# The rings of the split weights are moved by 16 bytes against the activations

## The reference

```python
def swiglu_ffn(h, w_gate_up, w_down):
    gate, up = jnp.split(h @ w_gate_up, 2, axis=-1)
    return (jax.nn.silu(gate) * up) @ w_down

def reference(x, ...):
    h = x
    for i in range(DEPTH):                      # DEPTH = 2
        kind, j = i % N_MIXERS, i // N_MIXERS
        if kind == 0:
            h = h + stick_breaking_mixer(rmsnorm(h, sb_norm[j]), sb_w_qkv[j], sb_w_o[j])
        elif kind == 1:
            h = h + chunked_gmlp_mixer(rmsnorm(h, gm_norm[j]), gm_w_in[j], gm_v_norm[j],
                                       gm_w_s[j], gm_b_s[j], gm_w_o[j])
        ...
        h = h + swiglu_ffn(rmsnorm(h, ffn_norm[i]), ffn_w_gate_up[i], ffn_w_down[i])
    return rmsnorm(h, final_norm)
```

## Time and profile before

| | |
|---|---|
| median of 2 runs | 2072.2 us (2070.47 to 2073.94) |
| the profiled execution | 2069.99 us |
| its span, first to last instruction | 2068.3 us |
| TensorE matmul busy | 2058.8 us |
| VectorE busy | 1430.0 us |
| ScalarE busy | 1011.4 us |
| granted TensorE clock, mean | 0.999 |
| moved by DMA | 402.47 MB, mean 195 GB/s |

### The profile page before, as it was taken

The page is one execution under the profiler, slowest core; times in us unless marked ns, Lnnn a source line. Parts: engine busy times, 40 slices in busy tenths (PEclk is TensorE's granted clock), DMA queues, the critical chain, the costliest instruction groups (busy, mean ns, idle before and its releaser), DMA issues.

```text
span 2068.3 us, 27155 instructions
## 1 busy us (share of the span) xinstructions
PE 2058.8 (100%) x9279; PEld 1721.7 (83%) x9279; DVE 1430.0 (69%) x1822; ACT 1011.4 (49%) x1285; POOL 16.4 (1%) x30
## 2 busy tenths in 40 slices
PE   9999999999999999999999999999999999999998
PEld 7888888888888888888888888888888888888887
DVE  7787787867766677666557887877766677665454
ACT  6677765544444444444445444554444444444443
POOL 1000000000000000000000000000000000000000
PEclk9999999999999999999999999999999999999999
DMA  8555655666666666556567665566666666655554
GB/s 276 183 188 158 188 187 172 199 198 195 195 191 200 195 197 195 195 194 201 195 196 211 193 203 186 191 194 204 195 191 202 194 198 196 191 198 201 194 194 152
DMA packets 207419, 402.47 MB, mean 195 GB/s; under 512 B 12336, under 2 KB 13056, under 8 KB 206976
## 3 DMA queue, kind: packets, MB, share of 16 engines
q1 hardware_dynamic: 206496, 398.11, 61.8%
q0 software_dynamic: 688, 3.18, 0.4%
q10 hardware_dynamic: 176, 0.40, 0.1%
HBM read 399.55 MB, written 2.10 MB: 194 GB/s over the span
## 4 chain that ended last, share of the span: by engine, by line
PE 99%; issue 0%; ACT 0%; DVE 0%; POOLq 0%; POOL 0%; DVEq 0%; ACTq 0%
PE acc L1101 65%; PE acc L1109 32%; PE tp L1205 1%; PE tp L1185 1%; PE tp L1334 0%; PE acc L1151 0%; PE tp L1117 0%; PE acc L1144 0%; PE acc L1377 0%; PE acc L1375 0%; PE acc L1376 0%; ACT xT L382 0%; PE tp L1193 0%; DVE h L1070 0%; ACT junk L640 0%
## 5 line engine op out<-in xcount | busy, mean ns | idle before, releaser
L672 DVE TENSOR_TENSOR w_lo<-raw,w_hi 128x1024 fp32r<-128x1024 f32 x750 | 915.7, 1224 | 560.5 <-ACT w_hi L364 558.6
L364 ACT ACTIVATE w_hi<-raw 128x1024 fp32r<-128x1024 f32 x750 | 791.7, 1059 | 894.7 <-PE acc L1109 889.9
L1101 PE MATMUL acc<-w_hi,xT 128*128 128x512 f32 x4080 | 996.9, 385 | 0.0
L1101 PEld LDWEIGHTS acc<-w_hi,xT 128*128 128x128 f32 x4080 | 762.6, 187 | 148.2
L1109 PE MATMUL acc<-w_lo,xT 128*128 128x512 f32 x2040 | 539.0, 385 | 0.0
L1109 PEld LDWEIGHTS acc<-w_lo,xT 128*128 128x128 f32 x2040 | 381.9, 187 | 74.1
L1101 PE MATMUL acc<-w_hi,hid_lo 128*128 128x512 f32 x944 | 364.4, 386 | 0.0
L1101 PE MATMUL acc<-w_hi,hid_hi 128*128 128x512 f32 x944 | 362.3, 384 | 0.0
L1109 PE MATMUL acc<-w_lo,hid_hi 128*128 128x512 f32 x944 | 249.5, 385 | 0.0
L1101 PEld LDWEIGHTS acc<-w_hi,hid_lo 128*128 128x128 f32 x944 | 176.9, 187 | 36.4
L1109 PEld LDWEIGHTS acc<-w_lo,hid_hi 128*128 128x128 f32 x944 | 176.7, 187 | 34.4
(11 more groups left out here) (117 smaller groups left out, 428.3 us busy)
## 6 DMA issues: line engine op xcount, KB each, us to landing
raw<-in_ffn_w_gate_up SPq DMA_DIRECT2D x352, 512.0 KB, 4.5
raw<-in_ffn_w_down SPq DMA_DIRECT2D x176, 512.0 KB, 3.7
raw<-in_sb_w_qkv SPq DMA_DIRECT2D x95, 512.0 KB, 4.3
raw<-in_gm_w_in SPq DMA_DIRECT2D x64, 512.0 KB, 4.5
raw<-in_sb_w_o SPq DMA_DIRECT2D x32, 512.0 KB, 4.2
raw<-in_gm_w_o SPq DMA_DIRECT2D x32, 512.0 KB, 4.1
h<-in_x SPq DMA_DIRECT2D x3, 512.0 KB, 8.8
gain_bc<-in_gm_v_norm POOLq DMA_DIRECT2D x1, 1024.0 KB, 6.2
```

The costliest lines, as they stand in the source:

```text
L364: nc.scalar.activation(w_hi[:, p % RING], raw[:, p % RING], ACT.Copy).then_inc(hi_ready, 1)
L672: nc.vector.tensor_tensor(w_lo[:, p % RING], raw[:, p % RING], w_hi[:, p % RING].bitcast(f32), ALU.subtract).then_inc(lo_ready, 1)
L1101: nc.tensor.matmul(swept(acc_at(chunk, r)), part[:, kt, rs], swept(w_hi[:, p % RING, k]), start=(kt == 0 and part is hi), stop=False)
```

## The change

`w_hi` and `w_lo` were two tensors of SBUF. Now they are two views into one tensor `parts`, which is 32 bytes longer than both together; w_hi begins 16 bytes (SKEW = LINE = 4 elements) into it and w_lo right behind w_hi. parts begins where w_hi began. raw, xT and h don't move, and region keeps a multiple of 512 bytes from parts. So the moving tiles begin 16 bytes beyond the place modulo 512 at which the stationary tiles begin. The tensors between w_lo and lead_in move by 32 bytes. No instruction is added, removed or put elsewhere.

```diff
         raw = sb("raw", [P, RING, KP, CH])
-        w_hi = sb("w_hi", [P, RING, KP, CH], f32r)
-        w_lo = sb("w_lo", [P, RING, KP, CH], f32r)
+        SKEW, SIZE = LINE, RING * KP * CH
+        parts = sb("parts", [P, 2 * SIZE + 2 * LINE], f32r)
+
+        def ring(first):
+            return parts[:, first:first + SIZE].rearrange("p (s k n) -> p s k n", s=RING, k=KP)
+
+        w_hi = ring(SKEW)
+        w_lo = ring(SKEW + SIZE)
         gate = sb("gate", [P, RT, CH])
...
         used_up_to = nc.lookup_mloc(moments).addr + 32
-        lead_in = sb("lead_in", [P, (nc.lookup_mloc(w_hi).addr - used_up_to) % CH // 4])
+        lead_in = sb("lead_in", [P, (nc.lookup_mloc(parts).addr - used_up_to) % CH // 4])
         region = sb("region", [P, 2 * KF * S])
         R0 = nc.lookup_mloc(region).addr
-        assert (R0 - nc.lookup_mloc(w_hi).addr) % CH == 0
+        assert (R0 - nc.lookup_mloc(parts).addr) % CH == 0
```

## The result

| | before | after |
|---|---|---|
| median of 2 runs | 2072.2 us | 2095.5 us (2095.32 to 2095.76) |
| span of the profiled execution | 2068.3 us | 2093.6 us |
| ratio to before | | 1.0113, 95% interval 1.0069 to 1.0156 |

The kernel became 1.1% slower, by 25.3 us in the spans. That is inside the stated range and within 2%, but it is a change: the interval leaves 1 out, and I had forecast 2072.

The account below looks back on a forecast made before the run. TensorE's matmul spacing, at full clock, was taken to bound the kernel. All terms were 0: 2070.0 + 0 = 2070 us for the profiled execution, the median 2.2 us over it, so 2072; range 2035 to 2105.

Parts of the forecast that it names:

- the spacing of 9024 matmuls: TensorE's 512-column matmuls on w_hi or w_lo start 223.5 ns apart, making 2017 us of the kernel.
- the splits on ScalarE and VectorE: Lines 364 and 672, making w_hi and w_lo from raw: 1059 and 1224 ns, off the path, priced at nothing.
- the small tensors: gate, res, gain_bc, ident and others move by 32 bytes; even 3 ns on some 52 transposes is 0.2 us; taken as 0.
- the DMAs: They write raw, which hasn't moved: 0.
- the pieces would show it: Groups of 12 matmuls begin every 2.68 us if the forecast holds, 2.72 second pattern, 2.62 or less faster, 2.74 or more slower.
- the mild slower case: Matmul stream rests somewhat worse but within 2%, 2087 to 2113 us; chance 0.11.
- the second pattern: Spacing of 226.5 ns instead of 223.5, seen from 141.31 to 157.62 us; everywhere it would add 27 us, 2099.
- the main term: Moving operand of 9024 matmuls one 16-byte line on: 0 ns; nearer bounds 27 us either way.
- The prediction's last sentence: The forecast is wrong if what matters is not how often the two operand streams meet but in which order.
- The second term: One plain-order matmul in every fourth piece, 188 times 0.03 us: 5.6 us either way, taken as 0.
- the slower rival: Matmul stream falls to a worse pattern; over 2% needs 228.1 ns spacing; chance 0.13, the splits included.
- The read ports: By the skill's rule of separate ports, no distance between rings and activations matters: 2070.0 us for the profiled execution.

Follow-up runs that it names:

- s0_moved_tensors: Changed kernel with the rings back on the multiple of 512 (SKEW = 0), one buffer and small tensors still moved: 2070.3 us, ratio 1.000 to the kernel before.
- raw16: Changed kernel with the raw ring moved by 16 bytes too: 2096.0 us, ratio 1.0127 to the kernel before.
- np0: Kernel before without any matmul in plain order (PLAIN = 0): 2094.6 us, ratio 1.0119.
- skew64: Changed kernel with the rings w_hi and w_lo moved by 64 bytes instead of 16, activations unmoved: 2062.7 us, ratio 0.9963 to the kernel before.
- skew256: Changed kernel with the rings moved by 256 bytes instead of 16, activations unmoved: 2070.2 us, ratio 1.000 to the kernel before.
- all64: Changed kernel with rings and activations (xT, hid_hi, hid_lo) all moved by 64 bytes: 2072.2 us, ratio 1.0007 to the kernel before.
- act64: Changed kernel with the rings back at 0 and only the activations moved, by 64 bytes: 2104.9 us, ratio 1.0166 to the kernel before.
- skew192: Changed kernel with the rings moved by 192 bytes instead of 16, activations unmoved: 2097.6 us, ratio 1.013 to the kernel before.
- skew80: Changed kernel with the rings moved by 80 bytes instead of 16, activations unmoved: 2124.9 us, ratio 1.0264 to the kernel before.
- act16: Changed kernel with the rings back at 0 and only the activations moved, by 16 bytes: 2120.4 us, ratio 1.0245 to the kernel before.
- np16: Changed kernel (rings at 16 bytes) without any matmul in plain order (PLAIN = 0): 2107.1 us, ratio 1.0179 to the kernel before.

## Why the prediction was wrong

**Right.** That the end hangs on nothing but the spacing of 9024 matmuls, and the price of a nanosecond in it (9 us): by the counts 2.9 ns more make 26 us, and the spans differ by 25.3. That the splits on ScalarE and VectorE, the small tensors and the DMAs cost nothing: s0_moved_tensors, raw16 and the two groups of 1224 and 1060 ns say so. That the pieces would show it, at full clock and without idle time. The value came out where the mild slower case stood (2087 to 2113, given 0.11), near the 2099 worked out from the second pattern's +3 ns; the spacing is 2.9 ns longer in the long stretches. That nearness is luck. By its mechanism it isn't that pattern: the stretch of the earlier trace rows runs in the seven steps that np0 keeps to, and these don't occur in the changed kernel's long stretches. There the stream is in cycles of 224.44 and 227.92 ns for a little under half of the steps each, and the mix happens to lie 3 ns up.

**The step that failed** is the one that set the main term to 0: "Seen from the stationary load the stream is the same, turned by one line of four", with "the number of meetings within a sweep stays". It argued from how often the two reads meet and took the pattern for something that lies within 64 bytes. skew64 (a move by 64 bytes) refutes it directly. By that argument a move of 64 bytes puts every sweep back on its place and must change nothing; it gave patterns of its own and 7 us less, and 128 bytes, no different in that view, gave 52 us more. For tiles on multiples of 64, and as far as the places tried show, the period is 256 bytes. The term that had been set to 0 was +12.5 us with the plain matmuls out of it. The prediction's last sentence had named the right doubt, that the order of the meetings might matter and not their number; no run shows the meetings themselves.

**The second term, mis-sized**, is the plain matmul: priced at its own length, 5.6 us either way, and taken as 0. It should have been priced by what it does. The earlier trace rows against the earlier trace rows had the price: it holds the stream 3 ns under the second pattern, 9024 x 3 = 27 us, and np0 measured 24.5. At the new place it is worth 11.5, so 13 us of the loss are this term's. The text had named this ("the resets by the plain matmul were seen to work for one distance") and then kept it for the rival alone.

**Two readings of the rows.** The prediction takes from the earlier trace rows that the plain matmul leads out of the second pattern. Those rows don't show it: the stream was in the four steps before and behind it, and the 0.03 us are the way back to them. In the stretch of the earlier trace rows it even fails twice, and later one does it. Steps in ns from the starts in the kernel before; the plain matmuls start at 143.8, 154.7 and 368.0 us:

```
143.8   220 235 239 225 226 220 221 221 P 233 226 235 227 219 233 225 226 220 222 221 234 239 225 226 ...
154.7   239 225 226 220 221 221 234 239 P 230 228 223 219 234 225 226 220 221 221 234 239 225 226 220 ...
368.0   225 226 220 222 220 235 239 225 P 226 220 230 224 221 218 230 224 221 218 230 224 221 219 230 ...
```

So in these three cases one plain matmul gets the stream out or doesn't, and they differ in the step of the cycle at which it comes. And "pieces worse than 2.72 aren't seen in the stretches read", used against the slower rival, was a misreading: the earlier trace rows gives only the mean of six, and one of them, from 152.17 to 154.91 us, takes 2.74.

```profile
152.17 1.97 PE L1101 MATMUL acc<-w_hi,xT 128*128 128x512 f32 x8
...
154.91 1.96 PE L1101 MATMUL acc<-w_hi,xT 128*128 128x512 f32 x8
```

Two slips in the sums change nothing: by the code there are 187 plain matmuls and not 188 (the last four pieces have none), and a spacing of 225 ns ends at 2086 us, not 2087.

**The inference on distance.** From equal means for xT and hid I concluded that large distances don't matter. True for multiples of 256, as skew256 shows; hid's two halves are 44 KB apart, a multiple of 256, so the rows had tested no distance under 256 bytes.

**The read ports.** The Trainium skill, "TensorE: Matmul & The Clock Gate", section "Step-by-step: what each phase is for", has the stationary load and the moving operand read through ports of their own, the load taking no read bandwidth from the running matmul. The measurement decides against the conclusion that the prediction let stand beside it, that no distance matters: the same instructions took 2048 to 2125 us by the places of the two operands and the resets. The runs don't show whether it is the ports or something behind them, memory or array, at which the two meet.

**Still open** is the mechanism itself: why the cycles have the steps that they have, why both tiles off a multiple of 64 is another case than both on one, and what a plain matmul resets. No run measured a matmul stream without stationary loads, or one with all matmuls in plain order. So that the load and the moving operand disturb one another is inferred from the two moves that undo one another (all64), and the part of the swept order is open.

## What to carry to other kernels

When TensorE is busy without gaps, compare starts: if equal matmuls stand at unequal but repeating distances, the place of the two operands in SBUF is a knob of some per cent (here 0.4% down to 2.7% up for moves of 16 to 192 bytes, and 1.1% down with the plain matmuls tuned to the place), and arguments on symmetry are no substitute for trying the few places. No simple rule came out of the places tried: the best was a distance of 64 bytes with both tiles on multiples of 64, but 128 bytes, on a multiple too, was among the dearest, together with 80 and the two moves of the stationary tiles to 16. What holds in another kernel has to be measured there. Anything tuned by phase, such as the plain matmuls here, has to be tuned again at each place: at 64 bytes the second plain matmul was worth 14.5 us, at 0 it cost about 1 (within the interval of no change), at 16 it cost 10.5.

## What the runs showed of the hardware that was not expected

- For tiles on multiples of 64 bytes the cycle depends on the distance of moving and stationary tile modulo 256: all64 and skew256 repeat the kernel before to the count (3134), act64 and skew192 one another in the first layer (3089), but not in the second (3059 and 3089).
- A stream of identical 512-column matmuls rests in cycles of 1 (mean step 220.0 ns, skew64), 2 (230.0, skew80), 4 (223.33, before), 5 (226.7, skew192), 6 (224.44, after), 7 (226.67, np0), 12 (229.4, act16) or 16 (227.92, np16) matmuls, the slowest at 231.7 ns (act64), at full granted clock. More than one cycle exists at one place, and a single matmul in another order of columns can move the stream between them.
- The patterns are no noise: s0_moved_tensors, all64 and skew256, three separate programs, show the steps of the kernel before, and their ratios to it are 1.000, 1.0007 and 1.000.
- The place of the rings changed next to nothing for ScalarE (1058 to 1063 ns for the copy) or VectorE (1223 and 1224 ns for the subtract) in any run.
